# A hybrid decoder block on eight cores: rotary score products of two key blocks on two 64-row halves of the matmul array

## The reference

```python
q = (rmsnorm(q_lat, q_a_g) @ w_q_b).reshape(b, s, 16, 192)        # 128 plain + 64 rotary dims a head
k_nope, v = split((rmsnorm(kv_lat, kv_a_g) @ w_kv_b).reshape(b, s, 16, 256), [128])
k = concat([k_nope, broadcast(k_rope)])                           # one 64-dim rotary key for all heads
q = apply_rope_tail(rmsnorm(q, q_norm_g), cos, sin)               # rot = [x1*cos - x2*sin, x2*cos + x1*sin]
k = apply_rope_tail(rmsnorm(k, k_norm_g), cos, sin)
y_mla = causal_block_attention(q, k, v) @ w_mla_out               # softmax(q k / sqrt(192)), causal
h = h + (gate_a * y_conv + gate_b * y_mla) @ w_o
h = h + (silu(a_gate) * a_up) @ w_ffn_down                        # a = causal conv of rmsnorm(h) @ w_ffn_up
```

## Time and profile before

| | us |
|---|---|
| median of 3 executions (lowest, highest) | 2418.32 (2418.03, 2421.03) |
| the profiled execution | 2421.73 |
| its span, first to last instruction, slowest core (core 2) | 2419.1 |
| spans of cores 0, 1, 2, 3 | 2405.6, 2405.7, 2419.1, 2398.1 |
| TensorE busy on core 2 | 2353.7 (97%) |

### The profile page before, as it was taken

How to read it: one execution, slowest core, us unless ns; L and a number is a source line. 1 busy time by engine, 2 the same in 40 slices (tenths; PEclk the granted TensorE clock), 3 DMA queues, 4 the chain that set the end, 5 groups by cost and what they waited for, 6 DMA issues and landing times.

```text
span 2419.1 us, 41786 instructions; the slowest of 8 cores (2397.2 to 2419.1 us)
## 1 busy us (share of the span) xinstructions
PE 2353.7 (97%) x13851; PEld 1245.3 (51%) x13900; DVE 1341.8 (55%) x2585; ACT 1094.4 (45%) x1877; POOL 172.6 (7%) x330
## 2 busy tenths in 40 slices
PE   4989999999999999999999999999999999999999
PEld 3874555555555555544444444444444444444444
DVE  3872777777777777761111112277457457547742
ACT  5953788888788878861111113333023113213310
POOL 1000000000000000000000000000100100110011
PEclk9999999999999999999999999999999999999999
DMA  9753121202020202144544457454554454455467
GB/s 221 167 97 64 20 40 24 40 19 50 14 50 14 50 10 50 49 98 90 83 80 82 83 125 170 70 88 76 77 93 80 73 92 81 73 90 87 78 111 153
DMA packets 65893, 188.34 MB, mean 78 GB/s; under 512 B 7616, under 2 KB 23232, under 8 KB 64512
## 3 DMA queue, kind: packets, MB, share of 16 engines
q0 software_dynamic: 46944, 140.56, 36.1%
q1 hardware_dynamic: 18720, 44.91, 5.6%
HBM read 310.20 MB, written 13.66 MB: 134 GB/s over the span
## 4 chain that ended last, share of the span: by engine, by line
PE 95%; DMA 2%; DVE 1%; ACT 1%; issue 1%; SPq 0%; ACTq 0%; DVEq 0%; POOLq 0%
PE ps L621 95%; ACT arena L628 1%; DMA arena<-wkvin 1%; DMA arena<-wall 1%; DVE arena L639 1%; DVE arena L635 0%; SPq L655 0%; ACT L628 0%; ACTq L187 0%; DVEq L187 0%; DVE arena L1098 0%; DVE arena L652 0%; POOLq L187 0%; SPq L187 0%
## 5 line engine op out<-in xcount | busy, mean ns | idle before, releaser
L621 PE MATMUL ps<-arena 128*128 128x476 bf16 (+7 forms) x13851 | 2353.7, 331 | 61.0 <-ACT arena L628 34.4
L621 PEld LDWEIGHTS ps<-arena 128*128 128x128 bf16 x13900 | 1245.3, 98 | 1169.1 <-issue 83.3
L639 DVE TENSOR_TENSOR arena<-ps,arena 128x476 f32<-128x476 f32 (+6 forms) x558 | 329.7, 591 | 776.3 <-PE ps L621 754.0
L639 DVE TENSOR_TENSOR arena<-arena 128x478 f32<-128x478 f32 (+18 forms) x1292 | 640.0, 536 | 196.2 <-ACT arena L628 174.0
L628 ACT ACTIVATE arena<-arena 128x476 f32<-128x476 f32 (+9 forms) x543 | 378.5, 712 | 683.8 <-DVE arena L639 607.6
L628 ACT ACTIVATE arena<-ps,arena 128x476 bf16<-128x476 f32 (+6 forms) x832 | 490.9, 631 | 410.2 <-PE ps L621 377.1
L635 DVE SCALAR_TENSOR_TENSOR arena<-arena 128x476 f32<-128x476 f32 (+8 forms) x603 | 358.2, 609 | 45.5 <-ACT arena L628 24.2
L628 ACT ACTIVATE arena<-ps 128x512 bf16<-128x512 f32 (+7 forms) x496 | 267.6, 561 | 117.5 <-PE ps L621 114.9
L655 POOL DMA_DIRECT2D arena<-wall x302 | 159.3, 528 | 2117.1 <-PE ps L621 2070.1
L635 DVE SCALAR_TENSOR_TENSOR arena<-ps,arena 128x256 bf16<-128x256 f32 (+1 forms) x65 | 27.1, 464 | 12.0 <-PE ps L621 7.3
L655 POOL DMA_DIRECT2D arena<-xg x23 | 12.5, 560 | 101.3 <-ACT arena L628 57.3
(11 more groups left out here) (3 smaller groups left out, 0.3 us busy)
## 6 DMA issues: line engine op xcount, KB each, us to landing
arena<-wall POOLq DMA_DIRECT2D x182, 512.0 KB, 5.5
arena<-wall POOLq DMA_DIRECT2D x48, 320.0 KB, 4.3
arena<-xg SPq DMA_DIRECT2D x9, 1024.0 KB, 6.9
arena<-wall POOLq DMA_DIRECT2D x32, 256.0 KB, 3.8
arena<-xg POOLq DMA_DIRECT2D x15, 512.0 KB, 10.2
arena<-xo SPq DMA_DIRECT2D x16, 477.0 KB, 13.8
outT<-arena SPq DMA_DIRECT2D x31, 238.0 KB, 5.3
arena<-wall POOLq DMA_DIRECT2D x32, 224.0 KB, 5.7
```

What stands on the lines that cost most here:

```text
L621: S.add(PE, lambda e: e.matmul(out, lhsT=lhsT, rhs=rhs, start=start, stop=stop), reads, writes, cost=max(width(rhs) / 2400.0, 0.055) + 0.003)
L639: S.add(DVE, lambda e: e.tensor_tensor(out=out, in0=in0, in1=in1, op=op), reads, writes, cost=dcost(out, in0, in1) + held)
```

## The change

- Queries are rotated outright. `QR` multiplies the raw rotary query by sine (`qsn`, table `SNq`) and cosine (`qrot`), four transfers on SP's queue (channels `qsw0` to `qsw3`) exchange the 32-row groups of the sine product into `qsw`, and DVE adds it. `QS` scales the 64 rows of its head into one half of `Qr`, and a transfer (`qd`) copies them to the other half. `krot` now copies the rotated key unchanged into rows 64 to 127, and builds the two tables with three more transfers (`tb0` to `tb2`).
- A score unit is now two key blocks: two plain products, then two rotary products of 64 rows each, the first on array rows 0 to 63 and the second on rows 64 to 127, then two exponentials. A head with an odd number of pieces ends with a single one.
- Scores use four banks (0 to 3) in turn, so bank 3 is no longer given to fillers; `PT` has 8 slots and `LA` is 5.
- `BOUNDS` becomes (0, 1212, 2280, 3230, 4096): shares of 1212, 1068, 950 and 866 rows.

```diff
@@ -371,7 +371,7 @@
 NKB = NKEY // 128
 
 
-BOUNDS = (0, 1220, 2290, 3242, 4096)
+BOUNDS = (0, 1212, 2280, 3230, 4096)
 
 
 class Share:
@@ -617,9 +617,9 @@
             n *= d
         return n
 
-    def mm(out, lhsT, rhs, start, stop, reads, writes):
+    def mm(out, lhsT, rhs, start, stop, reads, writes, share=1.0):
         S.add(PE, lambda e: e.matmul(out, lhsT=lhsT, rhs=rhs, start=start, stop=stop), reads, writes,
-              cost=max(width(rhs) / 2400.0, 0.055) + 0.003)
+              cost=max(share * width(rhs) / 2400.0, 0.055) + 0.003)
 
     ptr = lambda x: 0.0 if x is None or isinstance(x, (int, float)) else 1.0
 
@@ -1212,14 +1212,13 @@
         if F.at("qk") < 0:
             allowed = [6, 7] + [0, 1, 2] * (F.at("lout") >= NG - 1) + [3, 4, 5] * (F.at("qn") >= 0)
         else:
-            allowed.append(3)
             if i >= 0:
                 cs = pieces[i][0]
                 a, b = span[cs]
                 if a + 2 <= i <= b - 7 and F.at("fin") >= cs - 1:
                     allowed.append(4 + (cs + 1) % 2)
         allowed = [b for b in allowed if F.owner[b] == 0]
-        if stream is st_c and len([b for b in (3, 6, 7) if F.owner[b] == 0]) < 1:
+        if stream is st_c and F.owner[6] and F.owner[7]:
             return None, 0.0
         if not allowed:
             return None, 0.0
@@ -1262,8 +1261,10 @@
 
     def krot():
 
-        for r, q in ((64, 32), (96, 0)):
-            dma(SP, krope[r:r + 32, :], krope[q:q + 32, :], "krs%d" % q, reads=Tkr, writes=Tkr)
+        dma(SP, krope[64:128, :], krope[0:64, :], "krs", reads=Tkr, writes=Tkr)
+        dma(SP, SNq[0:64, :], CSq[64:128, :], "tb0", reads=[TCSq], writes=[TSNq])
+        dma(SP, SNq[64:128, :], CSq[64:128, :], "tb1", reads=[TCSq], writes=[TSNu])
+        dma(SP, CSq[64:128, :], CSq[0:64, :], "tb2", reads=[TCSq, TSNq, TSNu], writes=[TCSq])
 
     F.pos["lout"] = NG - 2 if NG % 2 else NG - 1
 
@@ -1295,14 +1296,15 @@
         v, t = P4.slabs(NKU, [512], BF16, "Kn%d" % i)
         Kn.append(v.rearrange("p a b -> p (a b)"))
         TKn.append(t)
-    Qn, TQn, Qr, TQr = [], [], [], []
+    Qn, TQn, Qr, TQr, TQd = [], [], [], [], []
     for i in range(2):
         v, t = P4.tile([NA], BF16, "Qn%d" % i)
         Qn.append(v)
         TQn.append(t)
-        v, t = P4.tile([NA], BF16, "Qr%d" % i)
-        Qr.append(v)
-        TQr.append(t)
+        o = P4.take(NA * 2)
+        Qr.append(V(o, [NA], BF16))
+        TQr.append([S.region(o + 2 * a, 2 * n, "Qr") for a, n in T3])
+        TQd.append([T("Qd") for _ in T3])
     for name, kind, k, nbytes in (("Q", "hq", 1, 4608), ("B", "hkv", 2, 2048)):
         ring(name, [P4.take(nbytes) for _ in range(k)], [nbytes] * k,
              [b for b, pl in enumerate(plan) if pl[0][0] == kind])
@@ -1315,13 +1317,18 @@
     sqr, Tsqr = P4.slabs(NT, [W], BF16, "sqr")
     rsqh, Trsqh = P4.tile([W], F32, "rsqh")
     qraw, Tqraw = P4.tile([W], F32, "qraw")
-    qrot, Tqrot = P4.slabs(NT + 1, [W], F32, "qrot")
+    qrot, Tqrot = P4.slabs(NT, [W], F32, "qrot")
+    qsn, Tqsn = P4.tile([W], F32, "qsn")
+    qsw, Tqsw = P4.tile([W], F32, "qsw")
+    Tqsx = [T("qsw%d" % i) for i in range(3)]
+    SNq, TSNq = P4.tile([NA], F32, "SNq")
+    TSNu = T("SNq")
     ast, Tast = P4.slabs(2, [NA], BF16, "ast")
     for i in range(2):
         v, t = P4.slabs(NVU, [512], BF16, "Vh%d" % i)
         Vh.append(v.rearrange("p a (b n) -> p (a b) n", n=128))
         TVh.append(t)
-    NPT = 6
+    NPT = 8
     PT, TPT = P4.slabs(NPT, [sh.CW], BF16, "PT")
     acc, Tacc = P4.slabs(4, [sh.CW], F32, "acc")
     accb, Taccb = P4.tile([sh.CW], BF16, "accb")
@@ -1434,11 +1441,14 @@
             for k in range(6):
                 mm(PS[p][:, 0:n], w[:, k, 256:384], qn[:, k, off:off + n], k == 0, k == 5, [Tw, Tqn[k]], [TP[p]])
             act(sqr[:, t, 0:n], PS[p][:, 0:n], AF.Square, [TP[p]], [Tsqr[t]])
-            for x, y in ((0, NT), (1, t)):
-                r = slice(64 * x, 64 * x + 64)
-                for o in (slice(0, 64), slice(64, 128)):
-                    tt(qrot[o, y, 0:n], PS[p][r, 0:n], CSq[o, off:off + n], ALU.mult, [TP[p], TCSq], [Tqrot[y]],
-                       0.09 * (o != r))
+            tt(qsn[:, 0:n], PS[p][:, 0:n], SNq[:, off:off + n], ALU.mult, [TP[p], TSNq, TSNu], [Tqsn])
+            tt(qrot[:, t, 0:n], PS[p][:, 0:n], CSq[:, off:off + n], ALU.mult, [TP[p], TCSq], [Tqrot[t]])
+            for x in range(4):
+                r = 32 * x
+                q = 32 * (x ^ 1)
+                dma(SP, qsw[r:r + 32, 0:n], qsn[q:q + 32, 0:n], "qsw%d" % x, reads=[Tqsn],
+                    writes=[Tqsx[x - 1] if x else Tqsw])
+            tt(qrot[:, t, 0:n], qrot[:, t, 0:n], qsw[:, 0:n], ALU.add, [Tqrot[t], Tqsw] + Tqsx, [Tqrot[t]])
 
         def QN(t):
             w, Tw = wget(("hq", h // 2))
@@ -1456,12 +1466,13 @@
         def QS(t):
             off, n = T3[t]
             p = fbank()
-            y = t if h % 2 else NT
+            r, d = (slice(64, 128), slice(0, 64)) if h % 2 else (slice(0, 64), slice(64, 128))
             mm(PS[p][:, 0:n], ones, sqn[:, 0:n], True, True, [Tones, Tsqn], [TP[p]])
             rsq(rsqh[:, 0:n], PS[p][:, 0:n], 192.0, [TP[p]], [Trsqh])
             stt(Qn[hb][:, off:off + n], qraw[:, 0:n], gqe, rsqh[:, 0:n], ALU.mult, ALU.mult,
                 [Tqraw, Tgqe, Trsqh], [TQn[hb]])
-            tt(Qr[hb][:, off:off + n], qrot[:, y, 0:n], rsqh[:, 0:n], ALU.mult, [Tqrot[y], Trsqh], [TQr[hb]])
+            tt(Qr[hb][r, off:off + n], qrot[r, t, 0:n], rsqh[r, 0:n], ALU.mult, [Tqrot[t], Trsqh], [TQr[hb][t]])
+            dma(SP, Qr[hb][d, off:off + n], Qr[hb][r, off:off + n], "qd%d" % t, reads=[TQr[hb][t]], writes=[TQd[hb][t]])
 
         def end(which):
             left[which] -= 1
@@ -1502,15 +1513,26 @@
     NKH = -(-sh.nkh // 4)
     KUN = NKH + (NKH + 1) // 2
 
-    def qk(i, b):
-        cs, h, kb, a, c0, c1 = pieces[i]
-        hb = h % 2
-        x = i % NPT
-        ks = slice(kb * 128, (kb + 1) * 128)
-        n = c1 - a
-        mm(PS[b][:, 0:n], Kn[hb][:, ks], Qn[hb][:, a:c1], True, False, [TKn[hb][kb // 4], TQn[hb]], [TP[b]])
-        mm(PS[b][:, 0:n], krope[:, ks], Qr[hb][:, a:c1], False, True, [Tkr[kb], TQr[hb]], [TP[b]])
-        act(PT[:, x, a - c0:c1 - c0], PS[b][:, 0:n], AF.Exp, [TP[b], Trkh[hb]], [TPT[x]], scale=rkh[hb][:, kb:kb + 1])
+    def qk(js):
+
+        for i in js:
+            cs, h, kb, a, c0, c1 = pieces[i]
+            hb = h % 2
+            mm(PS[i % NSB][:, 0:c1 - a], Kn[hb][:, kb * 128:(kb + 1) * 128], Qn[hb][:, a:c1], True, False,
+               [TKn[hb][kb // 4], TQn[hb]], [TP[i % NSB]])
+        for y, i in enumerate(js):
+            cs, h, kb, a, c0, c1 = pieces[i]
+            hb = h % 2
+            r = slice(64 * y, 64 * y + 64)
+            mm(PS[i % NSB][:, 0:c1 - a], krope[r, kb * 128:(kb + 1) * 128], Qr[hb][r, a:c1], False, True,
+               [Tkr[kb]] + TQr[hb] + TQd[hb], [TP[i % NSB]], 0.5)
+        for i in js:
+            cs, h, kb, a, c0, c1 = pieces[i]
+            act(PT[:, i % NPT, a - c0:c1 - c0], PS[i % NSB][:, 0:c1 - a], AF.Exp, [TP[i % NSB], Trkh[h % 2]],
+                [TPT[i % NPT]], scale=rkh[h % 2][:, kb:kb + 1])
+            F.mark("piece", i)
+            masks(i)
+            F.mark("mask", i)
 
     def masks(i):
         cs, h, kb, a, c0, c1 = pieces[i]
@@ -1603,14 +1625,12 @@
             n += 1
         u.pos = spans[n][0] + spans[n][1] * c / spans[n][2]
         c += u.pe
-    LA = 4
-
-    def step_s(i):
-        qk(i, i % 3)
-        F.mark("piece", i)
-        masks(i)
-        F.mark("mask", i)
-        F.pos["qk"] = i
+    LA = 5
+    NSB = 4
+
+    def step_s(js):
+        qk(js)
+        F.pos["qk"] = js[-1]
 
     def step_p(i):
         cs = pieces[i][0]
@@ -1624,10 +1644,10 @@
 
     free_ = lambda b: F.owner[b] == 0
 
-    def ok_s(i):
-        h = pieces[i][1]
-        return (kdone(h) and qdone(h) and F.at("piece") >= i - 3 and F.at("pv") >= i - LA - 1
-                and F.at("sum") >= i - NPT + 1 and free_(i % 3))
+    def ok_s(js):
+        h, i = pieces[js[0]][1], js[-1]
+        return (kdone(h) and qdone(h) and F.at("piece") >= i - NSB and F.at("pv") >= i - LA - 1
+                and F.at("sum") >= i - NPT + 1 and all(free_(j % NSB) for j in js))
 
     def ok_p(i):
         cs, h, kb = pieces[i][:3]
@@ -1639,8 +1659,11 @@
 
     for i, (cs, h, kb, a, c0, c1) in enumerate(pieces):
         w = where[i - NPH * h]
-        st_s.units.append(Unit(lambda i=i: step_s(i), 2 * (c1 - a) / 2400.0, room=[TP[i % 3]], ok=lambda i=i: ok_s(i),
-                               pos=h + w))
+        if (i - NPH * h) % 2 == 0:
+            js = [j for j in (i, i + 1) if j < NPH * (h + 1)]
+            n = sum(pieces[j][5] - pieces[j][3] for j in js)
+            st_s.units.append(Unit(lambda js=js: step_s(js), 1.5 * n / 2400.0, room=[TP[j % NSB] for j in js],
+                                   ok=lambda js=js: ok_s(js), pos=h + w))
```

## The result

The changed kernel takes 2577.9 us in its profiled execution, which is also its fastest; the ratio of its undisturbed executions to those of the kernel before is **1.0662** (95% interval 1.0636 to 1.0688), against 0.988 forecast. It is 6.6% slower, and outside the range.

What follows compares the result with a forecast made beforehand. TensorE's streamed columns bound the attention, the slowest of four cores setting the time. Columns with new bounds, minus pair overlap, plus 47 ns a mode change gave 2390 us, minus 0.8: 2389 us, 1.2% below 2418.3; range 2368 to 2440 us.

Steps and rivals of the forecast that it cites:

- step 3: Query preparation: DVE saves 0.65 us per `QR`, transfers land in 2.0 us, `qd` copies hidden; cost at the end nothing.
- step 4: PSUM banks: fillers lose bank 3, two banks suffice; nothing, at most a few us where short units meet.
- step 2: TensorE mode changes around half-array rotary products: 47 ns each, 16.5 us on core 0, 46.6 us on core 3.
- Step 1: TensorE columns streamed: paired rotary products save 18.1 us on core 0 to 81.7 on core 3; bounds alone give core 3 2424.0.
- the 77 ns at which I had said that it decides: TensorE mode changes: price per change at which core 3 reaches the span of before.
- the array empties at each change: Rival on TensorE mode changes: the array drains each time; at 166 ns core 3 takes 2507 us; chance 0.20 from 60 ns up.
- The range's upper end: Top of the forecast range over all cores: 2440 us, at 99 ns a change, with 0.16 of the chance above it.
- The late-exchange rival: Rival on the `QR` transfers: landing at 7.7 us costs TensorE 96 us on core 0, end 2485 us; chance 0.05.
- the test by which changes are cheap if core 0 is the slowest by far: Sign in the profile's core spans: core 3 slowest by far means dear mode changes, core 0 slowest means cheap ones.
- the named signs of being wrong: Change above 77 ns, halves taking turns, or TensorE's waits for DVE or ACT growing by tens of us.

Runs made afterwards that it cites:

- run 1: Changed kernel with both rotary products of a pair on the same array half, order of instructions unchanged; core 3 takes 2520.5 us.
- run 2: Changed kernel with rotary products on all 128 rows, second key half zeroed, no mode changes; ratio 1.0627, core 3 2422.1 us, core 0 2560.8.
- Run 14: Kernel before plus new bounds and rotated queries with transfers, score units standing back until the rotated query has landed; ratio 1.0025, core 0 2414.2 us.
- run 10: Kernel before with PSUM bank 3 taken from fillers during the attention; core 0 takes 2487.2 us.
- run 11: Kernel before with paired scores on four banks, `LA` 5, eight slots, banks 0 and 1 kept free for the first pair, whole array; ratio 1.0412, core 0 2509.9 us.
- run 12: Kernel before without bank 3 for fillers, the planner freeing a unit's bank after the last operation that reads it; ratio 1.0164, core 0 2454.6 us.
- run 3: Changed kernel with banks 0 and 1 kept from fillers before the first score; core 2 2427.0 us, core 0 2560.7, core 3 2460.4.
- run 15: Changed kernel with banks 0 and 1 kept free at the start, early bank release, and score units awaiting their rotated query; ratio 1.0291.
- run 9: Kernel before plus new bounds and rotated queries, DVE making the exchange and second copy instead of transfers; ratio 1.009, core 0 2436.2 us.

## Why the prediction was wrong, step by step

The measured time is core 0's, and what failed there are the copies of step 3 and the banks of step 4; step 2 by itself would have made core 3 the last, at some 2443 us.

- **Step 1 (columns) was right.** The saving was counted as 81.7 us on core 3, and run 1 measures 77; the bounds alone were to put core 3 at 2424.0, and run 2 has 2422.1. (One row ahead of it was misread: the 13.3 us of the earlier trace rows are idle time of the weight loader, not a wait of TensorE. Nothing in the sum rests on it.)
- **Step 2 (the price of a change) looked at the right term and mis-sized it:** 47 ns taken, 97 to 105 ns measured, above the 77 ns at which I had said that it decides. For a full pair of 434 columns that is 202 ns spent for 181 ns saved. The value came from one-column products in a stream, and was rough even for them: in the single records of the trace before they start 25 ns apart (418.913, 418.937 and 418.963 us on core 2). There the weights of a product load as soon as the product ahead of it has started; after the change the loader starts only 273 ns after the last whole product (601.108 against 600.835 us), so the new weights are not loaded ahead. The rival "the array empties at each change" was thus right for core 3 in what it costs, at 101 ns and not at its 166. The Trainium skill, TensorEngine Tiling (Array Packing), Key Properties, says that changing the mode drains TensorE; the trace shows a pause at every change and gives its length, but not what fills it. The emptying of the array and the late load of the weights are not told apart by any run here. The range's upper end, 2440 us, was worked out at 99 ns on core 3, and core 3 alone (2443.6) would have been just beyond it.
- **Step 3 (the query's preparation) failed on core 0, at the copies `qd`,** which it called hidden, since they end some 7 us before they are read. That is 15% of a head of about 50 us, which is core 2's; core 0 has 16 heads in some 450 us, 28 us each, and so some 4 us. The landing itself was forecast at 2.0 us and measured at 1.9, and DVE's waits for the exchange came as forecast (13 of them from 250 to 850 us, 28.8 us in all). But the planner counted a query as ready once its operations were issued, so it placed a head's first scores at once, ahead of fillers that could have run, and TensorE, which keeps its order, stood there 13 times, for 45.6 us in all and up to 7.2 us at a time. At 631.25 us, for one, the product starts 2.2 us after DVE has finished what is copied. Run 14 shows this as the cause, for the rotation by itself: telling the planner gives back 51 to 59 of 83 us. The late-exchange rival had a price of that order (96 us) but by a landing of 7.7 us that did not occur.
- **Step 4 (banks), "nothing", was wrong by 82 us on core 0** (run 10), and pairs add 23 (run 11; that they need two free banks at once is my reading, not tested). I had compared a bank's use by one convolution unit with its eviction, on core 2. In the program core 0's preparations come more often, since a head has only 21 pieces to hide them, and hold a bank through a chain of ACT and DVE operations. Early release gives back 33 us (run 12). The other 49 are, by the table above, mostly waits of TensorE for ACT and DVE (25.7 us more than before) and a lower clock; what makes these waits was not settled.
- **Not foreseen at all:** fillers that starve the first pair on core 2, 30 us (run 3). It needed no run: 192 filler units ahead of the first score stand in the order of the changed kernel.
- **The choice of core.** The sum took each core's columns and changes, but banks, landings and ACT were weighed on cores 2 and 3, where pieces are many; the shortest heads were the ones that broke. So the test by which changes are cheap if core 0 is the slowest by far misled: core 0 is the slowest by far, and changes are dear. Two of the named signs of being wrong did come: a change above 77 ns, and TensorE's waits for DVE and ACT, which grew by tens of us on core 0 (to 31.0 and 35.6, from 5.8 and 3.1).
- **Still open:** the cause of the 49 us of run 12; about 40 us on core 1, which run 15 leaves above the 2431.5 of the redone sum; the 45 us of run 9, where TensorE's waits for DVE are 33.8 us instead of 5.8 (DVE has more work there, which I argue but did not test).

## What to carry to other kernels

Price a change of the array's mode at about 100 ns each way before splitting products in two: a pair of half-array products that stands alone among whole ones pays only beyond some 480 columns (estimate: 202 ns at 2400 columns a us). When a share of the work has short heads, check banks and late operands there, not where TensorE is fullest; and when an engine keeps a fixed order, a landing of 2 us that the planner does not know of holds up all the work placed behind it, and the lower clock adds to the price. Before running, count in the new order how much filler stands ahead of the first unit that needs two resources at once.

## What was not expected of the hardware

Two 64-row products on different halves started 3 ns apart and overlapped nearly whole (77 of 81.7 us): the split itself works, and only passing between the modes is dear, 97 ns into the halves and 105 ns out of them, with no weights loaded ahead. The granted clock fell along with the lost density and made it worse: 1.00 where core 0's TensorE was busy 98 us of 100, and 0.88 (a mixture of 1.2 and 2.4 GHz) where it was busy 66, while cores 1, 2 and 3 of the die had 0.97, 1.00 and 1.00 in the same 100 us.
